# One scan in place of sixteen small vector instructions that build a row of 0 to 127

## The reference, cut to what matters

```python
def hierarchical_moe(h, w_rg, b_rg, w_re, b_re, w_gate, w_up, w_down):
    ...
    pg_top, g_idx = lax.top_k(pg, 1)
    e_sel = jnp.take_along_axis(e_logits, g_idx[:, :, None], axis=1)[:, 0]
    pe_top, j_idx = lax.top_k(pe, TOP_K)
    weights = pg_top * pe_top / jnp.sum(pe_top, axis=-1, keepdims=True)
    e_idx = g_idx * EXPERTS_PER_GROUP + j_idx
    ...
    for e in range(N_EXPERTS):
        act = jax.nn.silu(hf @ w_gate[e]) * (hf @ w_up[e])
        y = y + combine[:, e:e + 1] * (act @ w_down[e])
```

## Time and profile before

| | before |
|---|---|
| median of three runs | 1760.12 us |
| the profiled execution's own time | 1759.02 us |
| its span, first to last instruction | 1757.2 us |
| PE busy | 1615.4 us (92%) |
| DVE busy | 806.6 us (46%) |
| ACT busy | 539.3 us (31%) |

### The profile page before, as it was taken

How to read it: one execution, slowest core, us unless ns; L and a number is a source line. 1 busy time by engine, 2 the same in 40 slices (tenths; PEclk the granted TensorE clock), 3 DMA queues, 4 the chain that set the end, 5 groups by cost and what they waited for, 6 DMA issues and landing times.

```text
span 1757.2 us, 20158 instructions
## 1 busy us (share of the span) xinstructions
PE 1615.4 (92%) x8271; PEld 1204.8 (69%) x8271; DVE 806.6 (46%) x1390; ACT 539.3 (31%) x874; POOL 73.6 (4%) x90
## 2 busy tenths in 40 slices
PE   3999999999996999999999999999999994888786
PEld 3997777777785788888886687788678882333232
DVE  5456343355363666666223874426663615222111
ACT  5234443344432322222112433232353312111110
POOL 3000000000000000000000000000000001121111
PEclk9999999999998999999999999989999996999898
DMA  4334312112324356473222222121213518999994
GB/s 134 108 97 123 95 49 72 56 65 72 78 92 140 117 168 215 151 236 124 96 99 90 72 74 72 53 65 51 72 49 144 192 56 322 388 410 404 413 403 164
DMA packets 146128, 258.33 MB, mean 147 GB/s; under 512 B 16268, under 2 KB 120888, under 8 KB 132720
## 3 DMA queue, kind: packets, MB, share of 16 engines
q1 hardware_dynamic: 138512, 241.44, 38.9%
q0 software_dynamic: 7520, 15.56, 3.1%
HBM read 251.69 MB, written 15.23 MB: 152 GB/s over the span
## 4 chain that ended last, share of the span: by engine, by line
PE 84%; DVE 6%; issue 4%; DMA 3%; ACT 2%; SPq 0%; POOL 0%; POOLq 0%; DVEq 0%; ACTq 0%
PE psum L2291 20%; PE psum L2292 20%; PE psum L2293 20%; PE psum L2859 7%; PE psum L2876 3%; PE psum L2611 1%; PE psum L2600 1%; PE psum L2583 1%; PE psum L2837 1%; DMA Xg<-h_rows,tok 1%; DMA raw<-w_in 1%; PE psum L2504 1%; DVE WL L1453 1%; ACT Sb L1042 1%; PE psum L2356 1%
## 5 line engine op out<-in xcount | busy, mean ns | idle before, releaser
L2291 PE MATMUL psum<-AH,WH 128*128 128x512 f32 (+1 forms) x1240 | 490.6, 396 | 14.3 <-DVE AL L1499 6.3
L2292 PE MATMUL psum<-AL,WH 128*128 128x512 f32 (+1 forms) x1240 | 474.6, 383 | 0.0
L2293 PE MATMUL psum<-AH,WL 128*128 128x512 f32 (+1 forms) x1240 | 471.7, 380 | 0.0
L1453 DVE TENSOR_TENSOR WL<-raw,WH 128x2048 fp32r<-128x2048 f32 (+1 forms) x100 | 226.6, 2267 | 184.8 <-ACT WH L953 184.5
L2291 PEld LDWEIGHTS psum<-AH,WH 128*128 128x128 f32 x1240 | 235.4, 190 | 78.4 <-issue 20.1
L2293 PEld LDWEIGHTS psum<-AH,WL 128*128 128x128 f32 x1240 | 235.8, 190 | 46.2
L2292 PEld LDWEIGHTS psum<-AL,WH 128*128 128x128 f32 x1240 | 235.9, 190 | 43.7 <-issue 3.1
L953 ACT ACTIVATE WH<-raw 128x2048 fp32r<-128x2048 f32 (+1 forms) x100 | 189.0, 1890 | 141.3 <-PE psum L2293 107.5
L2859 PE MATMUL psum<-WE,XT 128*64 128x512 f32 x544 | 131.8, 640 | 15.6 <-issue 13.6
L2859 PEld LDWEIGHTS psum<-WE,XT 128*64 128x64 f32 x544 | 48.0, 147 | 97.3 <-issue 97.3
L2876 PE MATMUL psum<-WE,AT 128*64 128x512 f32 x272 | 63.7, 610 | 28.6 <-issue 27.0
(11 more groups left out here) (505 smaller groups left out, 1953.2 us busy)
## 6 DMA issues: line engine op xcount, KB each, us to landing
raw<-w_in SPq DMA_DIRECT2D x45, 1024.0 KB, 5.2
WE<-w_gate SPq DMA_DIRECT2D x34, 1024.0 KB, 17.9
WE<-w_up SPq DMA_DIRECT2D x34, 1024.0 KB, 27.6
WE<-w_down SPq DMA_DIRECT2D x34, 1024.0 KB, 28.2
araw<-w_ada SPq DMA_DIRECT2D x24, 1024.0 KB, 5.7
raw<-w_ffn_in SPq DMA_DIRECT2D x22, 1024.0 KB, 6.3
raw<-w_ffn_out SPq DMA_DIRECT2D x11, 1024.0 KB, 4.9
raw<-w_out SPq DMA_DIRECT2D x8, 1024.0 KB, 5.1
```

Of the source, the lines that this page charges most:

```text
L1453: V.tensor_tensor(WL[:, n, 0:w], raw[:, n, 0:w], WH[:, fed[0] % HL, 0:w].bitcast(F32), ALU.subtract).then_inc(S_("lo_ready"), 1)
L2291: MM(dst, lh, rh, start=first, stop=False)
L2292: MM(dst, lh, rl, start=False, stop=False)
L2293: return MM(dst, ll, rh, start=False, stop=last)
```

## The change

`iota` is now the result of one `tensor_tensor_scan` over the constant tile `ones` (128 ones, set by POOL at the start of the kernel): from a state of -1 it multiplies by one and adds one at each element, and so writes 0 to 127. The sixteen `tensor_scalar` instructions that wrote it are gone. `thr` reads `iota[:, 1:8]` where it read `expert[:, 1:8]`, and the comparison at line 2193 reads the first 30 numbers of `iota` where it read those of `expert`. The numbers are the same.

```diff
             def routing_numbers():
                 link(V.tensor_scalar(later, K("expert"), -1000.0, None, ALU.add))
-
-
-                spread = iota[:, 0:CAP].rearrange("p (a v) -> p a v", a=8)
-                for a_ in range(8):
-                    link(V.tensor_scalar(spread[:, a_, a_:], K("expert")[:, 0:8 - a_], 8.0, float(a_), ALU.mult, ALU.add))
-                    if a_:
-                        link(V.tensor_scalar(spread[:, a_, 0:a_], K("expert")[:, 8 - a_:8], 8.0, float(a_), ALU.mult, ALU.add))
-                link(V.tensor_scalar(iota[:, CAP:], iota[:, 0:CAP], float(CAP), None, ALU.add))
-
-                link(V.tensor_scalar(thr[:, 0, :], K("expert")[:, 1:8], float(CAP), 0.5, ALU.mult, ALU.add))
+                link(V.tensor_tensor_scan(iota, ones, ones, -1.0, ALU.mult, ALU.add))
+                link(V.tensor_scalar(thr[:, 0, :], iota[:, 1:8], float(CAP), 0.5, ALU.mult, ALU.add))
                 link(V.tensor_scalar(thr[:, 1, :], thr[:, 0, :], -1.0, None, ALU.add))
...
             at_pair = [P, 2 * NB, NPAIR]
-            link(V.tensor_tensor(here, K("expert", NPAIR).unsqueeze(1).to_broadcast(at_pair),
+            link(V.tensor_tensor(here, iota[:, 0:NPAIR].unsqueeze(1).to_broadcast(at_pair),
                                  pair.unsqueeze(2).to_broadcast(at_pair), ALU.is_equal))
```

## The result

The changed kernel takes 1771.27 us, the median of four runs (1770.13 to 1772.68); the execution that was profiled took 1773.78. The ratio to the kernel before is 1.0059, with a 95% interval from 1.0041 to 1.0077. No change was forecast, 1760.1 us in a range of 1758.0 to 1762.0; the time lies 9 us outside.

What follows compares the result with a forecast made beforehand. PE was taken as the bound, busy 1615.4 of 1757.2 us. DVE's 2.81 us saving ends in waits and the other edits cost 0, so 0 us on the path (-0.3 to +0.1): 1760.1 us, range 1758.0 to 1762.0.

Steps and rivals of the forecast that it cites:

- The stretch of the edit: Dense stage `wo2` near 1391 us: PE busy without a gap, so its start does not move; 0 us there.
- the saving on DVE: Sixteen instructions of 3.27 us replaced by one scan of 0.46 us: 2.81 us saved, bounds 2.0 to 3.0.
- the new idle time before an evacuation: DVE in `wo2`, before an evacuation into `hT`: idle 2 to 3 us more, waiting for PE.
- The other two edits: `thr` and the line 2193 comparison reading `iota`: same shape, so 0 us; comparison's bounds -0.04 to +0.04 us.
- That the saving reaches the end: Rival: PE idled unseen at the hand-over to ("wo2", 1), giving 1757.3 us; chance 0.04, wholly or in part.
- Slower by instruction fetch: Rival: DVE's shorter list shifts fetch places, hurting after 1450 us, up to 7.8 us (1767.9); chance 0.03 with other layout shifts.
- The serial stretch: DVE after 1450 us, on which token gathering waits: its comparison, 0.40 us long, keeps its length, 0 us.

Runs made afterwards that it cites:

- delay1: Changed kernel with one long reduction of about 3 us on DVE ahead of the scan: 1770.69 us, ratio 1.0061.
- in_order: Kernel before, no scan, the same sixteen instructions with operands that write 0 to 127 in order, comparison still reading the constant: 1771.35 us, ratio 1.0077.
- scan_first: Kernel before with the scan put ahead of the sixteen old instructions, which overwrite it: 1759.75 us, ratio 1.0002.
- scan_thr: Changed kernel with the comparison reading the constant row again, leaving the scan and `thr` edits: 1770.98 us, ratio 1.0059.
- here_only: Kernel before with one edit alone, the comparison reading the old `iota`; most token lists go wrong and row moves are left out: 1740.08 us, ratio 0.9886.
- same_after: The changed kernel, unchanged, timed again: 1770.37 us, ratio 1.0058.
- fill15: Changed kernel with fifteen of the sixteen old instructions put back ahead of the scan, which overwrites them: 1771.54 us, ratio 1.0066.
- by_engine: Kernel before with `iota` ordered so consecutive rows go to consecutive DMA engines under one supposed map of partitions to engines: 1759.12 us, ratio 1.0001.
- by_eight: Kernel before with iota[8a+v] = 8v+a in each half, so consecutive rows go to consecutive groups of eight partitions: 1777.85 us, ratio 1.0107.
- twice: Kernel before with the first small instruction of routing_numbers (`later`) written out twice: 1761.02 us, ratio 0.9998.

## Why the prediction was wrong

**The stretch of the edit** was read rightly. The scan was forecast at 0.42 us and took 0.42, the saving on DVE at 2.81 us and was 2.79, and the new idle time before an evacuation came as said. PE gained nothing: its first product of the slab stands 3.63 us late, as all the rest does there. `delay1`, which gives the saving back, has the changed kernel's time.

**The step that failed** is the premise that the numbers in `iota` are the same. Under "The other two edits" it put their price at 0 because the shape is the same, and line 2189, which reads `iota` to build the token lists, has no term in the sum at all. The runs show 12.2 us for the order of these numbers alone (`in_order`) and 0.6 us, within the noise, for the scan alone (`scan_first`); the comparison's edit costs nothing by itself (`scan_thr` has the changed kernel's time). I priced instructions by shape and place, and took the contents for equal after reading the loop as a slow way to write 0 to 127. The loop's own operands say otherwise: a factor of 8 on the inner index, the outer one added, and two pieces where one would do if no rotation were meant. Working out its first eight numbers (0, 8, 16, 24, ...) would have been enough to see it. The edit of the comparison rested on the same thing: with the old `iota` it would have gone wrong, as `here_only` shows.

**The rivals** were drawn from that premise too. That the saving reaches the end: `delay1` and `same_after` do not differ. Slower by instruction fetch: it had the right sign, 0.03 of the chance and the wrong cause; `fill15` refutes it. No rival looked at what the data of the routing do to the DMA, though the page of before shows the DMA engines busy 9 tenths or more in slice after slice near its end, where the experts are. This row of the 40 slices was the view left out:

```profile
DMA  4334312112324356473222222121213518999994
```

**The serial stretch** after 1450 us was forecast not to change. The comparison takes 0.40 us as before.

## What to carry to other kernels

An edit that replaces a table or an index by "the same thing, made faster" has two prices, that of the instructions and that of the values; write down the first few values of both before pricing the first. Where a gather or a scatter moves fewer rows than a tile has partitions, the order of rows over partitions sets which DMA engines do the work, and in a stage bound by DMA it is the busiest engine that counts. A spread order costs a few hidden instructions (`by_engine` needs three where the old loop needed sixteen) and evening out the two halves gave another 4 us.

## What the runs showed of the hardware

The order of the rows over the partitions, and with it the largest load of a DMA engine, set the time, and not the bytes: with the same 258.33 MB in the same 146128 packets, where the expert rows lie in their tiles alone moved the whole from 1755 to 1781 us. A group of partitions served by one engine is not a run of eight: an order that is even over such runs (`by_eight`) was 18.7 us slower, and one that is even over the sets p to p+3 with p+32 to p+35 (`by_engine`) lost nothing. In a scatter that runs alone, the engines without a row closed after 0.12 us and those with eight rows after 3 to 4 us. And the profiled execution of `twice` was 2.5 us late from its first 50 us on without a change in its median, so an offset of that size in one trace is no finding.
